# Another order of the latent attention, the queries and keys first, in the mixers of a two-block transformer; SyncE issues the modulation's loads

## The reference, cut to what matters

```python
def first_block(x, ...):
    h = layer_norm(x, ln0_g, ln0_b)
    for l in range(2):
        proj = h @ w_in[l]      # cq 384, ckv 256, kr 64, xp 256, xqk 256, xv 256, xo 256, ipre 4, fpre 4
        cq, ckv, kr, xp, xqk, xv, xo, ipre, fpre = jnp.split(proj, _split_points(), axis=-1)
        a = mla(cq, ckv, kr, ...)        # rms_norm(cq) @ w_uq and rms_norm(ckv) @ w_ukv, rotary,
                                         # causal softmax attention, 4 heads
        p = multiscale_pool(xp, ...)     # means over windows of 2, 4, 8, 16 tokens, a 64x64 product per group
        m = mlstm(xqk, xv, xo, ipre, fpre, ...)   # short convolution, q and k, gated scores, 4 heads
        mix = jnp.concatenate([a, p, m], axis=-1) @ w_out[l]
        h = layer_norm(ALPHA * h + mix, ln1_g[l], ln1_b[l])
        a, g = jnp.split(h @ w_up[l], 2, axis=-1)             # 2 x 2816
        g = causal_dwconv(g, w_fconv[l], b_fconv[l])          # width 3
        h = layer_norm(ALPHA * h + (silu(g) * a) @ w_down[l], ln2_g[l], ln2_b[l])
    return h

def second_block(x, c, ...):
    for l in range(2):
        mod = silu(c) @ w_ada[l] + b_ada[l]                   # [1, 1024] @ [1024, 6144]
        sh1, sc1, g1, sh2, sc2, g2 = jnp.split(mod, 6, axis=-1)
        # modulated norm, conformer convolution and banded attention, w_out_2, gated residual
        # modulated norm, dense swiglu (layer 0) or 8 experts with the top 2 (layer 1), gated residual
```

## Time and profile before

| part of the execution | from, us | to, us | TensorE busy, us |
|---|---|---|---|
| first norm | 0 | 24.26 | 7.24 |
| mixer, output and feed-forward of layer 0 | 24.26 | 394.93 | see the rows |
| mixer of layer 1 | 394.93 | 516.65 | see the rows |
| output and norm of layer 1 | 516.65 | 553.84 | 30.56 |
| feed-forward of layer 1 | 553.84 | 772.00 | 207.16 |
| second block, layer 0, attention and convolution | 772.00 | 945.00 | 143.61 |
| second block, layer 0, dense feed-forward | 945.00 | 1144.00 | 196.40 |
| second block, layer 1, attention and convolution | 1144.00 | 1321.50 | 153.40 |
| second block, layer 1, experts | 1321.50 | 2388.00 | 1044.17 |

### The profile page before, as it was taken

The page is one execution under the profiler, slowest core; times in us unless marked ns, Lnnn a source line. Parts: engine busy times, 40 slices in busy tenths (PEclk is TensorE's granted clock), DMA queues, the critical chain, the costliest instruction groups (busy, mean ns, idle before and its releaser), DMA issues.

```text
span 2388.5 us, 31839 instructions
## 1 busy us (share of the span) xinstructions
PE 2237.9 (94%) x12980; PEld 1939.0 (81%) x12980; DVE 1776.1 (74%) x2245; ACT 1415.4 (59%) x1982; POOL 171.9 (7%) x217
## 2 busy tenths in 40 slices
PE   6989998998998888999888999999999999999998
PEld 6769998877998777999877777777777777777776
DVE  6557876457877855666855888888888888888887
ACT  5345544445543745443745667676777777776775
POOL 1120112221013000102000000000000000000000
PEclk9879998888999898999997999999999999999999
DMA  6335665235666313667412788898888888898985
GB/s 230 112 133 194 233 231 215 90 130 172 241 214 243 135 69 117 230 226 255 171 53 106 275 321 347 310 349 338 336 337 329 343 323 352 317 350 318 352 333 196
DMA packets 89430, 574.91 MB, mean 241 GB/s; under 512 B 10048, under 2 KB 10176, under 8 KB 31040
## 3 DMA queue, kind: packets, MB, share of 16 engines
q1 hardware_dynamic: 74160, 516.55, 57.8%
q0 software_dynamic: 14112, 53.48, 6.5%
q10 hardware_dynamic: 1008, 2.79, 0.3%
HBM read 571.75 MB, written 1.05 MB: 240 GB/s over the span
## 4 chain that ended last, share of the span: by engine, by line
PE 68%; DVE 17%; ACT 10%; issue 2%; DMA 2%; POOL 1%; DVEq 0%; POOLq 0%; ACTq 0%
PE bank L459 34%; PE bank L1969 33%; DVE wlo L1301 9%; ACT whi L909 4%; DVE side L1415 2%; DMA side<-in_w_ada 2%; ACT arena L2089 1%; DVE arena L1620 1%; ACT hsh L2094 1%; ACT hT L941 1%; ACT arena L1136 1%; DVE XC L1374 0%; ACT midh L1125 0%; DVE XC L1316 0%; DVE HL L1382 0%
## 5 line engine op out<-in xcount | busy, mean ns | idle before, releaser
L1301 DVE TENSOR_TENSOR wlo<-ring,whi 128x1024 fp32r<-128x1024 f32 (+2 forms) x1002 | 1161.3, 1206 | 127.4 <-ACT whi L909 117.0
L909 ACT ACTIVATE whi<-ring 128x1024 fp32r<-128x1024 f32 (+2 forms) x1006 | 992.6, 1027 | 173.5 <-PE bank L1969 145.3
L459 PE MATMUL bank<-HH,whi 128*128 128x256 f32 x1648 | 483.2, 293 | 41.2 <-DVE wlo L1301 16.9
L459 PE MATMUL bank<-HH,wlo 128*128 128x256 f32 x1648 | 474.6, 288 | 0.0
L459 PE MATMUL bank<-HL,whi 128*128 128x256 f32 x1648 | 474.3, 288 | 0.0
L1969 PE MATMUL bank<-whi,xgh 128*128 128x512 f32 x896 | 366.2, 409 | 8.7 <-DVE wlo L1301 0.2
L459 PEld LDWEIGHTS bank<-HH,whi 128*128 128x128 f32 x1648 | 322.9, 196 | 54.2 <-issue 17.8
L1969 PE MATMUL bank<-whi,xgl 128*128 128x512 f32 x896 | 354.6, 396 | 0.0
L1969 PE MATMUL bank<-wlo,xgh 128*128 128x512 f32 x896 | 353.8, 395 | 0.0
L459 PEld LDWEIGHTS bank<-HL,whi 128*128 128x128 f32 x1648 | 323.9, 197 | 0.2
L459 PEld LDWEIGHTS bank<-HH,wlo 128*128 128x128 f32 x1648 | 323.7, 196 | 0.0
(11 more groups left out here) (267 smaller groups left out, 2650.3 us busy)
## 6 DMA issues: line engine op xcount, KB each, us to landing
ring<-in_moe_gate SPq DMA_DIRECT2D x112, 1024.0 KB, 6.1
ring<-in_moe_up SPq DMA_DIRECT2D x112, 1024.0 KB, 5.6
ring<-in_moe_down SPq DMA_DIRECT2D x112, 1024.0 KB, 5.4
side<-in_w_ada POOLq DMA_DIRECT2D x96, 512.0 KB, 4.1
ring<-in_w_up SPq DMA_DIRECT2D x44, 1024.0 KB, 5.8
ring<-in_w_in SPq DMA_DIRECT2D x32, 1024.0 KB, 4.9
ring<-in_w_down SPq DMA_DIRECT2D x32, 704.0 KB, 5.4
ring<-in_ffn_gu SPq DMA_DIRECT2D x22, 1024.0 KB, 5.2
```

Source lines behind the costliest of these rows:

```text
L459: return pe.matmul(out, lhsT, rhs, start=start, stop=stop, skip_group_check=True)
L909: a.activation(hi, part, ACT.Copy).then_inc(*made.up(("hi", n, i)))
L1301: v.tensor_tensor(lo, part, hi.bitcast(F32), ALU.subtract).then_inc(*done.up(("lo", n, i)))
```

## The change

SyncE issues the loads of `w_ada`, between those of the ring: two at the start, and then one with each ring chunk whose slot comes from a chunk named in `stepped`. GpSimd's generator is gone; `acc_lo` is made by VectorE, and so is the low part of `w_out` 0. A group takes ten steps instead of eleven on every engine: `acc_hi` is called in the step of the eighth slice.

The mixer's order on TensorE becomes: `w_in` 1, 2, 3; the sums of squares of `cq`; `w_in` 4; the sums of squares of `ckv`; `q1`; `w_v`; `q2`; `w_xp`; the gates; `w_uq`, `w_uk`; `w_in` 0; the attention scores; `qk`; `acol`; `pool`; four times `selh` and `sc`; `w_in` 5; `num`; `w_uv`; `pT`; `pv`; `hmT`. The programs of ScalarE and VectorE and the order of the chunks follow. The first `w_out` chunk takes its parts in the order 4, 5, 0, 1, 2, 3, 6, 7. Seven steps of the modulation lie in a mixer, none in `w_out`, and none in the last output of `w_down` and `ffn_down`.

The diff, cut to its core:

```diff
--- before.py
+++ after.py
...
+            for c in range(1, 5):
+                chunk(("w_in", l, c), t["w_in"][l, c], (8, 256), "col")
             chunk(("w_v", l), t["w_v"][l], (8, 264), "k")
-            for c in range(5):
-                if c == 3:
-                    chunk(("w_xp", l), t["w_xp"][l], (8, 128), "k")
-                chunk(("w_in", l, c), t["w_in"][l, c], (8, 256), "col")
-            chunk(("w_mqk", l), t["w_mqk"][l], (5, 256), None)
-            chunk(("w_in", l, 5), t["w_in"][l, 5], (8, 256), "col")
+            chunk(("w_xp", l), t["w_xp"][l], (8, 128), "k")
             for c in range(2):
                 chunk(("w_uq", l, c), t["w_uq"][l, c], (3, 384), None)
             chunk(("w_uk", l), t["w_uk"][l], (2, 512), None)
+            chunk(("w_in", l, 0), t["w_in"][l, 0], (8, 256), "col")
+            chunk(("w_mqk", l), t["w_mqk"][l], (5, 256), None)
+            chunk(("w_in", l, 5), t["w_in"][l, 5], (8, 256), "col")
             chunk(("w_uv", l), t["w_uv"][l], (2, 512), None)
             for c in range(4):
                 chunk(("w_out", l, c), t["w_out"][l, c], (8, 256), "col")
...
-
-        BY_POOL = {CH["w_out", l, 0] for l in range(DEPTH)}
-
         def lo_made(n, i):
-            return g_lo("lo", n, i) if n in BY_POOL else v_lo("lo", n, i)
+            return v_lo("lo", n, i)
...
-                        for _ in range(10):
+                        for _ in range(9):
                             yield
                         b = take("mod", l, g, until=[(v_mod, "mod", l, g)])
-                        pe.wait_ge(*g_mod("lo", l, g))
+                        pe.wait_ge(*v_mod("lo", l, g))
...
+                pair(("w_in", l, 1), src, [(a_proj, "cqs0", l)])
+                next(mod)
+                pair(("w_in", l, 2), src, [(a_proj, "xp1", l)])
+                next(mod)
+                pair(("w_in", l, 3), src, [(a_proj, "ckvs", l)])
+                next(mod)
...
+                sums(("q_sums", l), a_proj("cqs1", l), (0, 1, 2), [(a_mla, "dev_q", l)])
+                pair(("w_in", l, 4), src, [(v_proj, "rot", l, "kr")])
+                next(mod)
+                sums(("kv_sums", l), a_proj("ckvs", l), (4, 5), [(a_mla, "dev_kv", l)])
+                spread(("q1", l), RS[:, 1, :], [(v_mla, "cq", l)], v_mla("diag", l, 0))
...
+
+                pair(("w_in", l, 0), src, [(a_proj, "xqk", l)])
+                next(mod)
...
+                n = CH["w_mqk", l]
...
+                b = take("acol", l, until=[(a_lstm, "floor", l)])
...
+                b = take("pool", l, until=[(a_proj, "pool", l, 1)])
...
+                for h in range(4):
+                    b = take("selh", l, h, until=[(v_lstm, "ex1", l, h)])
+                    pe.wait_ge(*v_lstm("M", l))
+                    mm(b[:, 0:S], C("selh")[0:4, 128 * h:128 * h + 128], MM, True, True).then_inc(*p_lstm.up(("selh", l, h)))
+                    b = take("sc", l, h, until=[(v_lstm, "sc", l, h)])
...
+                pair(("w_in", l, 5), src, [(a_proj, "xo", l)])
+
+                for i in range(2):
+                    b = take("num", l, i, until=[(v_lstm, "hm", l, i)])
...
-                b = take("hmT", l, until=[(v_lstm, "gated", l, 1)])
...
+                b = take("hmT", l, until=[(v_lstm, "gated", l, 1)])
+                pe.wait_ge(*v_lstm("hm_normed", l))
...
+                    single(("w_out", l, c), lambda k: v_mix("mix", l, k), lambda m: [(v_res, "out", l, 2 * c + m)],
+                           (4, 5, 0, 1, 2, 3, 6, 7))
...
-                    next(mod)
...
-                    downs(("w_down", l), m, [(v_res, "down", l, m)], lambda: next(mod))
+                    downs(("w_down", l), m, [(v_res, "down", l, m)], lambda: next(mod) if m < 7 else None)
...
-                        for _ in range(8):
+                        for _ in range(7):
...
-                ahead(CH["w_v", l])
+                split(CH["w_in", l, 2])
+                b = PS[BANK["w_in", l, 1]]
+                a.wait_ge(*p_w("w_in", l, 1, 1))
+                proj(("cq0", l), cq[:, 0:2, :], two(b[:, :]))
+                proj(("cqs0", l), SQ[:, 0:2, :], two(b[:, :]), ACT.Square)
+                next(mod)
...
+                split(CH["w_v", l])
+                a.wait_ge(*p_mla("q_sums", l))
+                a.activation(dev4[:, 0:2], PS[BANK["q_sums", l]][:, 0:2], ACT.Sqrt, bias=C("eps6"), scale=1.0 / 384).then_inc(
+                    *a_mla.up(("dev_q", l)))
+                a.wait_ge(*p_mla("kv_sums", l))
+                a.activation(dev4[:, 2:4], PS[BANK["kv_sums", l]][:, 0:2], ACT.Sqrt, bias=C("eps6"), scale=1.0 / 256).then_inc(
+                    *a_mla.up(("dev_kv", l)))
+
+                next(mod)
...
+                next(mod)
+                split(CH["w_in", l, 0])
+                a.wait_ge(*p_w("w_xp", l, 1))
+                proj(("xp0", l), XP[:, 0, 16:272], PS[BANK["w_xp", l]][:, 0:S])
+                next(mod)
+                a.wait_ge(*v_lstm("nab", l))
...
+                split(CH["w_in", l, 5])
...
+                soften((0, 1))
...
+                soften((2,))
...
-                for c in range(2):
-                    a.wait_ge(*p_mla("uq", l, 2 * c + 1))
...
+                split(CH["w_out", l, 0])
+                b = PS[BANK["pool", l]]
+                a.wait_ge(*p_mla("pool", l))
+                for m in range(2):
+                    proj(("pool", l, m), RAW[:, 4 + m, :], b[:, S * m:S * m + S], scale=W(f"s_pool{l}", m))
+                a.wait_ge(*p_w("w_in", l, 5, 1))
...
+                proj(("xo", l), XO[:, :, :], two(PS[BANK["w_in", l, 5]][:, :]), ACT.Sigmoid)
...
+                    if h == 1:
                         a.wait_ge(*v_lstm("centred", l))
                         a.activation(HM2, HM, ACT.Square).then_inc(*a_lstm.up(("hm2", l)))
...
-                        yield
+                        v.wait_ge(*a_mod("hi", l, g))
+                        v.tensor_tensor(acc_lo[:, :], side_acc, acc_hi[:, :].bitcast(F32), ALU.subtract).then_inc(
+                            *v_mod.up(("lo", l, g)))
...
+                split(CH["w_in", l, 2])
+                next(mod)
+                split(CH["w_in", l, 3])
+                next(mod)
+                split(CH["w_in", l, 4])
+                next(mod)
+                split(CH["w_v", l])
+                v.wait_ge(*a_mla("dev_q", l))
+                v.reciprocal(inv4[:, 0:2], dev4[:, 0:2]).then_inc(*v_mla.up(("inv_q", l)))
+                v.wait_ge(*v_mla("inv_q", l))
+                diagonal(inv4[:, 0:2], RS[:, 1, :]).then_inc(*v_mla.up(("diag", l, 0)))
+                v.wait_ge(*a_mla("dev_kv", l))
...
+                split(CH["w_xp", l])
...
+                next(mod)
+                split(CH["w_in", l, 0])
                 next(mod)
...
+                v.wait_ge(*p_mla("uq", l, 5))
+                rotated(l, PS[BANK["uq", l, 2]], QP, "qp", "kr")
+                v.wait_ge(*a_proj("xqk", l))
...
                 next(mod)
...
+                split(CH["w_in", l, 5])
+                ends, causal = [], C("causal")
...
+                    if h == 0:
+                        ends[2]()
...
+                split(CH["w_out", l, 0])
+                for m in range(2):
+                    low_of_mix(4 + m, RAW[:, 4 + m, :], ("mix", l, 4 + m))
...
+                for h in range(4):
+                    low_of_mix(h, PS[BANK["pv", l, h]][:, 0:S], ("mix", l, h))
...
-                    next(mod)
...
-                        next(mod)
+                        if m < 7:
+                            next(mod)
...
-            def modulation():
-                for l in range(DEPTH):
-                    for gr in range(6):
-                        for k in range(8):
-                            n = 8 * (6 * l + gr) + k
-                            if n >= 2:
-                                g.wait_ge(*v_mod("acc", n - 2))
-                            g.dma_start(side_in[n % 2], t["w_ada"][l, gr, k]).then_inc(s_side[n % 2], 16)
-                            yield
-                        yield
-                        g.wait_ge(*a_mod("hi", l, gr))
-                        g.tensor_tensor(acc_lo[:, :], side_acc, acc_hi[:, :].bitcast(F32), ALU.subtract).then_inc(
-                            *g_mod.up(("lo", l, gr)))
-                        yield
-                        yield
-                while True:
-                    yield
...
-                for _ in range(3):
-                    next(mod)
-                split(CH["w_out", l, 0])
...
+            def modulation():
+                for n in range(96):
+                    if n >= 2:
+                        sp.wait_ge(*v_mod("acc", n - 2))
+                    sp.dma_start(side_in[n % 2], t["w_ada"][n // 48, n // 8 % 6, n % 8]).then_inc(s_side[n % 2], 16)
+                    if n > 0:
+                        yield
+                    if n % 8 == 1:
+                        yield
+                        if n > 8:
+                            yield
```

(16 more changed lines are left out.)

383 lines of the change are left out of this document (147 added, 236 removed).

## The result

The kernel after takes 2393.78 us (median of 19 runs, 2389.28 to 2396.84) where the kernel before, over the same rounds, takes 2389.76. The ratio is 1.0022, with a 95% interval of 1.0015 to 1.003: 0.2% slower, where the forecast was 2372, 0.7% faster.

The account below looks back on a forecast made before the run. TensorE's own work bounds layer 0's feed-forward; the mixers also lose to idleness and low clock. From 2390.28 us, -4.3-8 (mixers) -6.8-2 (output stages) -4.4 (`w_down` ends) +5+1.9 (feed-forwards) = -18.6: 2372 us, range 2357 to 2387.

Parts of the forecast that it names:

- The mixers and the output stage: Mixers: reordering removes idleness and low clock, -4.3 and -8 us; output stages: modulation steps leave, -6.8 and -2 us.
- The bank hold: Mixer: the fourth head's `sc` waits for `pool`'s PSUM bank until ScalarE copies it, +5.4 us idle.
- the sentence that up to the scores there is no wait: Mixer, `w_in` 1 to 4 through `w_in` 0, ahead of the attention scores: no wait found.
- End of `w_down` and the norms: No accumulation before the last residual, so the norm's sums start 0.9 us late instead of 3.12: -2.2 us per layer.
- SyncE's queue: Side loads following weight loads in one queue cost 0 us; bounds -3 (landing waits vanish) to +36.
- the rival of the late side loads: `w_down` and `ffn_down`: side loads land 9.5 us after issue, making accumulations late, 36 us, total 2408 us; chance 0.06.
- +5 for waits: Feed-forwards, mainly `w_up`: `acc_hi` in the eighth accumulation's step holds ScalarE's split, four waits of 1.7 us and one about 3.
- the wait behind the end of `w_up`: Layer 0, j 21: two high parts stand behind `acc_hi`, a wait of about 3 us.
- slack of over 2 us per step on ScalarE: 0: `w_down` and `ffn_gu`: ScalarE's slack per step absorbs the earlier `acc_hi`, cost 0 us.
- `acc_lo` itself [...]: hidden: Feed-forward: `acc_lo` takes VectorE 1.2 us in a step without an accumulation, so it costs nothing.
- The likeliest case: Whole kernel: the forecast sum of -18.6 us holds, giving 2363 to 2378 us; chance 0.45.
- signs named for being wrong: Mixers lasting under 108 or over 121 us, or VectorE waiting for side loads in `w_down`.

Follow-up runs that it names:

- the first edit: The kernel after, with ScalarE's `acc_hi` made one step later, groups still of ten steps: 2371.58 us, ratio 0.993 to the kernel before.
- the second: The kernel after, with TensorE's modulation step in `w_down` and `ffn_down` behind the chunk's products instead of ahead: 2376.27 us, ratio 0.9945 to the kernel before.
- both: The kernel after, with `acc_hi` one step later and TensorE's modulation step behind the chunk's products: 2363.48 us, ratio 0.9891 to the kernel before.
- a third without any wait: New mixer order with the modulation as before and ScalarE's `pool` copies ahead of the exponentials: 2370.12 us, ratio 0.9923 to the kernel before.

## Why the prediction was wrong, step by step

- **The mixers and the output stage: right in size, and the terms mostly; but not shown to be the order's.** Forecast -12.3 for the mixers, measured -9.4 between the profiled executions; -8.8 for the output stages, measured -12.2, the more because the mean clock of the one in layer 0 rose from 0.85 to 0.95. The old order with the new modulation has mixers 8.0 us shorter than before, so most of the -9.4 needs no new order, and that the sum of the new order's steps came near it is in part luck. The bank hold was forecast at 5.4 us and measured at 4.96 and 5.09, `qk` at 3.4 and measured at 3.28. Wrong was the sentence that up to the scores there is no wait: with the new modulation VectorE's rotation behind the mLSTM's scans held them for 1.9 to 3.2 us in every trace until it was moved. In most of the traces of the new order the scores then have 20 to 24 us at half speed, counted in windows of a microsecond, against 17 in before; the trace of after has 17 in layer 0. Its mixer lasted 113.0 us there and 117.2, 115.4, 118.1 and 117.5 in four other kernels, which may account for the 4 us by which its execution lies below the median; that is not shown.
- **End of `w_down` and the norms: right.** The sums start 0.97 us late instead of 3.12 (forecast 0.9).
- **SyncE's queue: right that it costs nothing**, and the rival of the late side loads is refuted by the 0.0 us above. That the waits for landings vanish stood only among the bounds, as -3; VectorE's went from 14.5 us to none, and how much of that reached TensorE was not measured by itself. The Trainium skill's page "DMA: Bandwidth & Descriptors", section "Queues, rings and completion order", says that each DMA engine consumes its ring's descriptors in order, by which the side load lands no sooner than the weight load ahead of it. The trace agrees: each of the 96 side loads landed after the weight load ahead of it, by 1.2 us or more. The 9.5 us, the sum of the two times, were my estimate and not the page's; the median measured is 3.6, with most side loads issued 1.2 to 3.5 us after the weight load ahead of them. So the order holds here and the sum of the two times doesn't.
- **The feed-forwards: the step that failed.** The prediction put +5 for waits and +1.9 for the products; the windows show +28.7 (`w_up` +1.0 and +3.3, `w_down` +12.6 and +2.7, `ffn_gu` +0.7, `ffn_down` +8.4). The mechanism was named: `acc_hi` in the step of the eighth accumulation. And its four waits in `w_up` were forecast at 1.7 us and came at 1.80. Three things were mis-sized or missed. First, the wait behind the end of `w_up` was taken at 3 us; it is 5.29 us of idleness, ended by `acc_lo` and not by a split, and half speed for some eight more. Second, "slack of over 2 us per step on ScalarE: 0" for `w_down` and `ffn_gu`: slack of the mean step doesn't help when ScalarE and VectorE wait for each other in turn within one step, and the two engines' queues behind that were not walked through. Third, "`acc_lo` itself [...]: hidden" asked only whether VectorE had time, not who waits for `acc_lo`: in `w_down` TensorE's step stands ahead of its chunk, and in groups of ten it comes one step sooner behind the eighth accumulation than in before, so it wanted `acc_lo` at once (1.46, 2.26, 2.44 and 1.69 us of idleness). And none of these waits was priced with the low clock behind it. So the loss has two causes that meet: `acc_hi` a step early, and TensorE's products too near behind the eighth accumulation. The first moved back gave 22 us, the second 17.5, both 30. The waits in `w_up` need only the first, and it alone cost 27 us in the kernel before. The 11.1 us of `w_down` in layer 1 and of `ffn_down` needed both, since either edit takes them away nearly whole. Of the 12.6 us of `w_down` in layer 0 the first edit gave back nothing and the second 7.4; with both it still lasts 71.5 us against 66.9 in before, and has a wait of 2.71 us ended by a split.
- **The likeliest case** therefore lost its -18.6 to terms of my own sum. None of the signs named for being wrong appeared: the mixers lie within 108 to 121 us, and VectorE waits for no side load in `w_down`. And 12 us was too wide a bound for what can be told from none: the 0.2% measured is clear of 1. The slower rival that I did put, the side loads, had the right place (`w_down`) and the wrong cause.

## What to carry to other kernels

When a step is pulled forward into the same turn as what it waits for, look at what stands behind it on its engine and at who waits for that: two engines that fed a third side by side begin to take turns, and the sum of their mean slack says nothing. Walk through that one turn instruction by instruction, at each kind of place where it can fall (in the middle of a loop, at the seam between two loops), and look for the slow stretch behind each new wait of a matrix engine (here 5.29 us of idleness with eight more at half speed). Two changes that are good by themselves can cure the same wait, so price a bundle by one run of each part.

## What the hardware showed that was not expected

- A subtraction of GpSimd (128x1024, 2.35 us) stretched VectorE's two halves beside it from 2.36 to 3.67 us. The 1.3 us more are nearly the 1.45 us that GpSimd's still had to run when VectorE's began (259.87 and 2.35 us against 260.77), as if VectorE had waited for its end; the rows give only the total of the two halves. In the two `w_up` making it on the busier VectorE (1.22 us) was the cheaper choice, by 6.8 and 5.6 us.
- With 2.16 us of idleness ahead of the attention scores' rotary part the mean granted clock of the scores was 0.59, without it 0.70, in the same layer, and the same 50 products took 18.74 us against 14.98. Both are single traces, and a third without any wait had 18.98 us: what sets where the low stretch begins stays open.
- 512 KB loads issued by SyncE between ring loads landed in 3.6 us, and in 4.1 when GpSimd issued them; of the 14.5 us that VectorE had waited for them none were left.
